# Hybrid attention: probabilities scaled by GpSimd, outputs copied by ScalarE, scores on row halves of the array, values on column halves

## The reference, cut to what matters

```
lg_c = einsum(qa, kc_c) * scale;  p_cmp = masked_softmax(lg_c + bias)    # compressed keys: 15
lg_s = einsum(qa, ks_g) * scale;  p_s   = masked_softmax(lg_s + bias_s)  # selected keys (here all)
lg_w = einsum(qa, kwin) * scale;  p_w   = masked_softmax(lg_w + bias)    # window keys
o_a = g[0] * (p_cmp @ vc_c) + g[1] * (p_s @ vs_g) + g[2] * (p_w @ vwin)
lg_b = where(valid_b, einsum(qb, kbw) * scale + bias_b, NEG)             # banded, with a sink
m = maximum(max(lg_b), sink);  e = exp(lg_b - m)
o_b = (e / (sum(e) + exp(sink - m))) @ vbw
out = concatenate([o_a, o_b]) @ w_out
```

## Time and profile before

| | us |
|---|---|
| time, median of 3 runs | 3504.17 (3500.81 to 3507.8) |
| profiled execution, its own time | 3509.27 |
| its span, from the first instruction to the last | 3507.5 |
| attention stage in it, from the first staging of queries to the first instruction of `out2` | 1849.5 to 2011.18 |
| busy in the span: PE, DVE, ACT, POOL | 2892.5, 1526.5, 452.8, 886.6 |
| mean granted clock of TensorE | 0.903 |

### The profile page before, as it was taken

How to read it: one execution, slowest core, us unless ns; L and a number is a source line. 1 busy time by engine, 2 the same in 40 slices (tenths; PEclk the granted TensorE clock), 3 DMA queues, 4 the chain that set the end, 5 groups by cost and what they waited for, 6 DMA issues and landing times.

```text
span 3507.5 us, 25672 instructions
## 1 busy us (share of the span) xinstructions
PE 2892.5 (82%) x9302; PEld 1717.2 (49%) x9302; DVE 1526.5 (44%) x2316; ACT 452.8 (13%) x1020; POOL 886.6 (25%) x633
## 2 busy tenths in 40 slices
PE   5999887989999999999997899477776666666666
PEld 3444656478888884444456647133332222222222
DVE  5664364122210000001016704765666667767765
ACT  1000232011011010001005501000010001100000
POOL 2111100000000000000000002554556566666663
PEclk9999878999999999999988999798897887888788
DMA  9999420356544443444640045999999999999998
GB/s 380 395 401 341 124 83 15 120 197 222 201 147 155 155 148 140 155 150 137 218 136 1 2 145 218 418 384 417 379 401 422 422 421 422 408 422 422 422 421 355
DMA packets 232373, 922.71 MB, mean 263 GB/s; under 512 B 17819, under 2 KB 37475, under 8 KB 160355
## 3 DMA queue, kind: packets, MB, share of 16 engines
q0 software_dynamic: 99840, 637.57, 44.3%
q1 hardware_dynamic: 132181, 283.96, 23.8%
q10 hardware_dynamic: 272, 0.13, 0.0%
HBM read 918.41 MB, written 8.44 MB: 264 GB/s over the span
## 4 chain that ended last, share of the span: by engine, by line
PE 55%; DMA 25%; DVE 11%; POOL 4%; issue 2%; ACT 2%; DVEq 0%; POOLq 0%; SPq 0%; ACTq 0%
PE ps L1219 17%; PE ps L907 11%; DMA arena<-in_peer_v,proj 10%; PE ps L1245 9%; PE ps L1444 6%; DMA proj<-in_peer_v,proj 4%; DMA proj<-in_peer_u,proj 4%; DMA ring<-in_w_in 3%; DMA arena<-in_w_mod 3%; PE ps L1028 3%; POOL arena L487 3%; PE ps L1421 2%; DVE proj L2049 1%; POOL proj L487 1%; DVE arena L2049 1%
## 5 line engine op out<-in xcount | busy, mean ns | idle before, releaser
L1444 PE MATMUL ps<-proj,gates 128*128 128x512 f32 x992 | 576.0, 745 | 394.2 <-DMA proj<-in_peer_v,proj 272.2
L1219 PE MATMUL ps<-hT,ring 128*128 128x256 f32 x2816 | 608.2, 379 | 1.5 <-ACT hT L526 1.5
L1444 PEld LDWEIGHTS ps<-proj,gates 128*128 128x128 f32 x992 | 233.3, 243 | 733.6 <-issue 604.3
L1219 PEld LDWEIGHTS ps<-hT,ring 128*128 128x128 f32 x2816 | 535.0, 190 | 74.9 <-issue 2.2
L487 POOL DMA_INDIRECT proj<-in_peer_u,proj x128 | 204.8, 1600 | 1427.6 <-DVE proj L2042 1265.1
L907 PE MATMUL ps<-ring,hT 128*128 128x512 f32 (+2 forms) x960 | 381.7, 558 | 8.7 <-DMA ring<-in_w_in 8.7
L2049 DVE CUSTOM_DVE_ANT_0 arena<-arena,yT 128x2048 f32<-128x2048 f32 x128 | 291.5, 2291 | 211.4 <-DMA arena<-in_peer_u,proj 210.9
L2049 DVE CUSTOM_DVE_ANT_0 proj<-proj,yT 128x2048 f32<-128x2048 f32 x128 | 292.1, 2291 | 126.8 <-DMA proj<-in_peer_u,proj 122.7
L1245 PE MATMUL ps<-ring,arena 128*128 128x512 f32 x704 | 304.1, 595 | 2.7 <-ACT arena L725 2.7
L907 PEld LDWEIGHTS ps<-ring,hT 128*128 128x128 f32 x960 | 175.6, 194 | 214.5 <-issue 192.6
L1444 PE MATMUL ps<-arena,gates 128*128 128x512 f32 x512 | 237.3, 607 | 35.9 <-DMA arena<-in_peer_v,proj 35.7
(11 more groups left out here) (410 smaller groups left out, 2568.3 us busy)
## 6 DMA issues: line engine op xcount, KB each, us to landing
arena<-in_w_mod POOLq DMA_DIRECT2D x96, 1024.0 KB, 12.4
ring<-in_w_in SPq DMA_DIRECT2D x52, 1024.0 KB, 12.1
ring<-in_ffn_w_gate SPq DMA_DIRECT2D x44, 1024.0 KB, 5.2
ring<-in_ffn_w_up SPq DMA_DIRECT2D x44, 1024.0 KB, 5.2
ring<-in_ffn_w_down SPq DMA_DIRECT2D x44, 1024.0 KB, 4.8
ring<-in_w_out SPq DMA_DIRECT2D x32, 1024.0 KB, 5.2
ring<-in_peer_wq SPq DMA_DIRECT2D x16, 1024.0 KB, 10.9
ring<-in_w_in SPq DMA_DIRECT2D x16, 960.0 KB, 18.2
```

The source lines that it names most:

```text
L1219: ins = pe.matmul(ps[:, 4 * m + f, 0:T], ring[:, s, k, P * f:P * (f + 1)], hT[:, KS * s + k, :], start=(s == 0 and k == 0), stop=(s == SLO ...
L1444: ins = pe.matmul(ps[:, 4 * t + b, :], diag[:, j, :], row_slots[n % ROWS][:, NB * b:NB * (b + 1)], start=(h == 0 and j == 0), stop=(h == H ...
```

## The change

Five things are changed, all in the attention stage.

- GpSimd takes the multiplication of the probabilities (`scaled`, waits on a new semaphore `att_fac` that `weigh` posts, posts `att_p`), and the staging of the queries (`q_in`).
- ScalarE takes `attended`, after `turned_out` of units 0 and 1 of the next pair; its loop does two pairs per turn, for the two halves of a query buffer that alternates between pairs. `q_out` is one instruction of 128 partitions in place of two of 64.
- The queries of the two heads lie together on 128 partitions, without zeros. A score product uses the row half of its head. Two units are scored together: in `half_scores(u, 0)` the first head of u and the second head of u + 1, in `half_scores(u, 1)` the others, so that the two products of one call go to different halves of the rows and to different banks of PSUM. TensorE waits on its own semaphore `first_half` between the two.
- The products with the values have 64 columns of weights and write to one half of the partitions each, alternating between halves.
- On TensorE all eight pairs are written out, without loops. The queries' tile need not be zeroed (L1903).

```
+        def scaled(i, past, u):
+
+            t, br = UNITS[u]
+            n = {"cmp": (7, 15)[t]}.get(br, P * (t + 1))
+            pool_eng.wait_ge(*at("att_fac", at_unit(i, past, u + 1)))
+            p = hyb["p"][:, u % 4, :, 0:n]
+            pool_eng.tensor_tensor(p, p, hst["sum"][:, u, :].unsqueeze(2).to_broadcast([P, 2, n]), ALU.mult).then_inc(sem("att_p"), 1)
+
+        def head_pair(i, past, more=True):
+            for u in range(NU):
+                scaled(i, past, u)
+                if u == 0 and more:
+                    pool_eng.wait_ge(*(at("att_turned", at_unit(i, past, -3)) if past else at("q_turned", 1)))
+                    q_in(i, past + 1)
...
-        def q_out(k):
-            for h in range(2):
-                r = slice(DK * h, DK * (h + 1))
-                ins = act.activation(hyb["q"][r, k, h, :], ps[r, 4 + k, T:2 * T], ACT.Copy, scale=DK ** -0.5)
-            ins.then_inc(sem("q_out"), 1)
+        def q_out(pair, k):
+            act.activation(hyb["q"][:, pair % 2, k, :], ps[:, 4 + k, T:2 * T], ACT.Copy, scale=DK ** -0.5).then_inc(sem("q_out"), 1)
...
+        def attended(i, past, k, u):
+            act.wait_ge(*at("att_pv", at_unit(i, past, u + 2)))
+            act.copy(yT[:, bass.ds(i + (past + 8 * k), 1), :], ps[:, 6 + k, 0:T].unsqueeze(1)).then_inc(sem("att_out"), 1)
...
+            r = slice(DK * h, DK * (h + 1))
+            ins = pe.matmul(ps[:, u % 4, T * h:T * h + n], hyb["q"][r, (past + u // NU) % 2, int(br == "ban"), P * t:P * (t + 1)], keys[r], start=True, stop=True)
+            if second:
+                ins.then_inc(sem("att_score"), 1)
+            return ins
+
+        def half_scores(i, past, u, n):
+
+            for v, h in (((u, 0), (u + 1, 1)), ((u, 1), (u + 1, 0)))[n]:
+                ins = score(i, past, v, h, n)
+            return ins
...
             for u in range(NU):
-                if u + 4 < NU or more:
-                    score(i, past, u + 4)
+                ahead = u % 2 and (u + 3 < NU or more)
+                if ahead:
+                    half_scores(i, past, u + 3, 0).then_inc(sem("first_half"), 1)
                 turn_p(i, past, u, more)
+                if ahead:
+                    pe.wait_ge(*at("first_half", i * 4 + (4 * past + u // 2 + 3)))
+                    half_scores(i, past, u + 3, 1)
...
             if br == "ban":
                 link(vec.tensor_tensor(s, s, hst["esink"][:, u, :], ALU.add))
-            link(vec.reciprocal(s, s))
-            if br != "ban":
+                link(vec.reciprocal(s, s), "att_fac", wait=False)
+            else:
                 gate = hst["gate"][:, 3 * t + ("cmp", "slc", "win").index(br), bass.ds(i * 2 + 2 * past, 2)]
-                link(vec.tensor_tensor(s, s, gate, ALU.mult))
-            p = hyb["p"][:, u % 4, :, 0:n]
-            link(vec.tensor_tensor(p, p, s.unsqueeze(2).to_broadcast([P, 2, n]), ALU.mult), "att_p", wait=False)
+                link(vec.reciprocal(s, s))
+                link(vec.tensor_tensor(s, s, gate, ALU.mult), "att_fac", wait=False)
```

More of the change, by code:

```diff
@@ L789, in head_pair @@
                 turned_out(i, past, u, more)
+                if u < 2 and past:
+                    attended(i, past - 1, u, NU - 2 + u)
         head_pair(0, 0)
-        with act.Fori(0, 6) as i:
+        with act.Fori(0, 6, 2) as i:
             head_pair(i, 1)
+            head_pair(i, 2)
         head_pair(0, 7, False)
+        for k in range(2):
+            attended(0, 7, k, NU - 2 + k)
         act.wait_ge(*at("att_out", 17))
@@ L1287, in _, with score @@
         pe.wait_ge(*at("kv_out", 1))
-        def score(i, past, u):
+        def score(i, past, u, h, second):
             t, br = UNITS[u % NU]
             g = kv_head(past, u)
-            if past or u >= 4:
+            if not second and (past or u >= 4):
                 pe.wait_ge(*at("att_exp", at_unit(i, past, u - 2)))
-            if u in (NU, NU + 3):
+            if not second and u in (NU, NU + 3):
                 pe.wait_ge(*at("q_out", i * 2 + (2 * past + 3 + u // (NU + 3))))
[L1297 to L1306, removed]
+            if br == "cmp":
+                n = (7, 15)[t]
+                keys = hyb["kc"][:, g, 0:n]
+            else:
+                n = P * (t + 1)
+                keys = hyb["kT"][:, 2 * ("slc", "win", "ban").index(br) + g, 0:n]
+            r = slice(DK * h, DK * (h + 1))
[7 more added lines that the diff above has]
+            return ins
         def turn_q(k):
@@ L1338, in values @@
             dst = ps[:, 7 if br == "ban" else 6, P * t:P * (t + 1)]
[L1339 to L1342, removed]
+            last = br in ("cmp", "ban")
+            for k in range(1 if br == "cmp" else t + 1):
+                for h in range(2):
+                    out = dst[DK * h:DK * (h + 1)]
                     if br == "cmp":
                         n = (7, 15)[t]
-                        v, w = hyb["v_cmp"][0:n, g, cols], hyb["pT"][0:n, u % 2, h, :]
+                        ins = pe.matmul(out, hyb["v_cmp"][0:n, g, DK:2 * DK], hyb["pT"][0:n, u % 2, h, :], start=False, stop=True)
                     else:
-                        v, w = hyb["v"][:, ("slc", "win", "ban").index(br), 2 * k + g, cols], hyb["pT"][:, u % 2, (t + 1) * h + k, :]
-                    ins = pe.matmul(dst, v, w, start=first, stop=(br in ("cmp", "ban") and h == 1 and (br == "cmp" or k == t)))
+                        ins = pe.matmul(out, hyb["v"][:, ("slc", "win", "ban").index(br), 2 * k + g, DK:2 * DK], hyb["pT"][:, u % 2, (t + 1) * h + k, :],
+                                        start=(br in ("slc", "ban") and k == 0), stop=(br == "ban" and k == t))
             ins.then_inc(sem("att_pv"), 1)
@@ L1366, in _ @@
         pe.wait_ge(*at("q_out", 2))
[L1367 to L1376, removed]
+        for u in (0, 2):
+            half_scores(0, 0, u, 0).then_inc(sem("first_half"), 1)
+            pe.wait_ge(*at("first_half", u // 2 + 1))
+            half_scores(0, 0, u, 1)
+        for pair in range(8):
+            head_pair(0, pair, pair < 7)
         values(0, 7, NU - 1)
@@ L1974, in head_pair @@
                     row_max(i, past, u + 3)
-                if u == 0 and more:
-                    vec.wait_ge(*(at("att_turned", at_unit(i, past, -3)) if past else at("q_turned", 1)))
-                    q_in(i, past + 1)
-                if u == 1 and past:
-                    attended(i, past - 1, 1, NU - 1)
-            attended(i, past, 0, NU - 2)
         vec.wait_ge(*at("bias_in", 16))
-        q_in(0, 0)
         for u in range(3):
```

31 lines of the change are left out of this document (15 added, 16 removed).

## The result

The kernel with the change took 3545.49 us, the median of 4 runs (3542.6 to 3549.32); the kernel before, beside it, 3505.91 (3500.81 to 3507.8). The ratio is 1.0116, 95% interval 1.0098 to 1.0133: slower by 39.6 us. The forecast was 3530, range 3508 to 3550. The way it moved and the relay were right; the size was +26 in place of +39.6. The time lies near the upper edge of the range: just outside the 3514 to 3545 that the forecast's own terms allow, inside only because the range reached towards the rival with a low clock throughout.

A forecast was written before the change was run, and what follows sets the result against it. VectorE's queue was taken as the bound, TensorE close behind. Pairs +4.1, +14.5 and +1.9, start -2.2 gave +18.3 us; low clock +8 made +26, so 3504.2 + 26 = 3530, range 3508 to 3550.

The forecast's parts named there:

- the relay: Attention pairs: four times, VectorE waits for scores behind TensorE's turn, which waits for GpSimd's multiplication; 9.5 us a pair.
- rival with a low clock throughout: Attention stage: relays plus TensorE at its low clock throughout, +43 us, 3547; chance 0.18.
- VectorE is relieved, and waits instead: Attention pairs: VectorE loses 7.1 us of work a pair, but idles before its bias step, about 75 us in all.
- The relay's price at full clock: Units 1, 3, 5, 7: handovers, GpSimd multiplication, turn and two passes cost 2.19, 1.92, 2.52, 2.46 us.
- Turn and scores do not flow into each other: TensorE in relays: scores start only when the turn has ended, not 0.16 earlier; a tiling change costs 0.18 us.
- The halves overlap, and it does not help: TensorE's scores: overlapping row halves give nothing in relays, since the head VectorE waits for is issued first.
- The clock: Attention pairs: TensorE busy 65% at most, so half the pairs' time at the low level, +8 us, bounds 0 and 17.
- First halves in the way of the turns: TensorE: values, first halves and even turns lie beside VectorE's 12.9 us and cost nothing at full clock.
- price at the low clock: Attention pairs: the four relays grow by 0.6, 0.3, 0.65 and 0.55 at the low level, 2.1 us a pair.
- No change: Rival: handovers of 0.05 and no drain make relays about 7.2 us, close to the 7.1 taken away; 3500 to 3508, chance 0.12.
- faster: Rival: GpSimd at VectorE's speed, short handovers and no drain make relays 4.9 us a pair; 3488, chance 0.08.
- the halves run one after the other: TensorE's array halves do not overlap; stays hidden and gives the same 3530; no separate chance.

The follow-up runs named there:

- e2: Kernel before plus only the moves to GpSimd and ScalarE; TensorE's full-width products and order as before: 3461.83 us, ratio 0.9879.
- e7: e2's kernel with scores of the next two units made only after the turn behind units 1, 5, 7, full width: 3513.19 us, ratio 1.0025.
- e5: e2's kernel with the values multiplied in column halves, scores still full: 3459.69 us, ratio 0.9878 to the kernel before.
- e1: Changed kernel with both halves of the scores issued ahead of the turn of unit u: 3517.34 us, ratio 1.0038 to the kernel before.
- e6: e1's kernel with values back to full width, row halves of the scores kept: 3506.69 us, ratio 1.0003 to the kernel before.

## Why the prediction was right, and where its size was off

**VectorE is relieved, and waits instead.** Right. VectorE's idle time at the bias step behind scores was forecast at about 75 us, 1.8 to 3 each; it was 92.9 us in 30 waits over the whole stage, 2.2 to 3.9 each (the first scores of the stage, which are no relay, not counted). The relief was forecast at 7.1 us a pair; e2 shows 20.0 - 14.1 = 5.9, with 0.7 of waits for scores left. The 20.0 held 0.4 that came from the loop's first pair alone; the others took 19.3 to 19.7.

**The relay's price at full clock.** Right, as far as it can be told. The change's own relays were never seen at full clock; e7 gives 2.38 to 2.54 in its cleanest pair for relays that by the same parts, with a whole unit's scores, were priced at 2.62 to 2.74. The parts, against the forecast: handover from VectorE to GpSimd 0.08 (0.15), from GpSimd to TensorE 0.15 (0.15); GpSimd's multiplication 0.61 and 1.04 (0.73 and 1.05); the two copies of `q_in` 0.74 together (0.8), so `scaled(1)` was on time.

**Turn and scores do not flow into each other.** The prediction took 0.18 from one row for the change between full and part of the array. e5 and e7, both at full clock, tell it better: two turns of `128*7` or `128*128` and then values start 0.22 apart where all is full width, 0.31 apart where the values are in column halves.

```profile
1921.88 0.38 PE L1362 MATMUL ps<-tab,proj 128*7 128x128 f32 x2 [0.91 <-POOL proj L496]
1922.10 0.61 PE L1384 MATMUL ps<-arena 128*128 128x128 f32 x4
```
```profile
1896.41 0.38 PE L1361 MATMUL ps<-tab,proj 128*128 128x128 f32 x2
1896.72 0.66 PE L1382 MATMUL ps<-arena 128*64 128x128 f32 x8
```

The 0.09 is half of what was taken. (The prediction counts 32 such changes in relays; by its own count of relays they are 30. The sum does not use it.) The Trainium skill, TensorEngine Tiling (Array Packing), section Key Properties, has the rule that a change of tiling mode drains TensorE: the trace agrees in direction. In the change itself, at the low clock, the scores start 0.07 ahead of the turn's end (1941.61 against 1940.57 + 1.11), where the prediction had 0, and 0.16 in a row of equal ones.

**The halves overlap, and it does not help.** e1's eight passes of 256 columns in row halves took 2.52 us at the low clock, against 1.91 for four at full width, so two units take 2.52 in place of some 3.8 (an estimate, twice the 1.91). The prediction said that this stays out of VectorE's way, since the head it waits for is first. Right.

**The clock: the step that failed.** The prediction reasoned from the busy share ("65% at most") to "half of the pairs' time at the low level: +8, bounds 0 and 17". TensorE had the low level nearly throughout (0.52 over seven pairs, five of them at 0.50), so the term was near its upper bound. The reasoning was too short as well: it has the clock follow from how busy TensorE is, and expects a slow TensorE, being a busy one, to be granted more again. In e1 it was busy 91% and stayed at 0.56; in e7, without halves, busy 77%, it had 0.88. And with the same order as e1's, the values at full width alone bring 0.56 to 0.84 (e6). So the busy share alone does not foresee the clock, and which products run matters too; the prediction did not consider that. Whether 65% at full width would have cost the clock in this stage, no run tests: there TensorE was never busy less than 74% of a pair in the loop. Elsewhere in the kernel before, 480 to 500 us, it had 58% and 0.64. What the low clock costs was in the rival of a low clock throughout, priced at +43 and given 0.18. Its time, 3547, is within 2 us of what was measured: the rival describes this result better than the forecast does.

**First halves in the way of the turns: priced at nothing.** "TensorE's other work (values, first halves, even turns) lies beside VectorE's 12.9 us and costs nothing at full clock". At the low clock it does cost: the turn of unit 1 started 0.61 later than it could, that of unit 7 0.25 (GpSimd done at 1946.34, turn at 1946.74). The rival had it, at 1 us a pair.

**The sum, mended.** In the loop the forecast was 22.4 + 1.05 = 23.45 us a pair, measured 25.7. Of the 2.2 between them, 1.05 is the other half of the clock's term; 0.9 is the relays' excess over their price at the low clock (2.44, the mean of 2.20 and 2.67, with 3.46, 3.28 and 3.30 are 12.5 against 11.6), which is the first halves; 0.3 is VectorE's own work beside the relays. Six pairs: 13.4 us. The first pair is 1.1 over its forecast with half a clock's term, and the last pair with the tail some 3, since its two relays, turns and values ran at 1.2 GHz too. With the start's -0.5 that is 17 us, the 43.3 - 26 of the stage.

**The other rivals.** No change and faster fell: relays are 2.2 us and more, GpSimd is about as slow as its rows said. That the halves run one after the other falls too, by the 2.52 above.

## What to carry to other kernels

- A unit of work may be moved to an idle engine only if nobody waits for the way there and back. Look at what the relieved engine does next, and behind what that stands in the third engine's queue: here the order `score(u + 4)` ahead of `turn_p(u)` makes the same moves worth -43 us (e2), and three relays a pair take all of it back (e7, 9 us above the kernel before). To issue it ahead of the turn of the same unit is not enough if the turn of the unit before still stands in its way (e1, e6).
- Fewer and shorter instructions on the array are not a gain by themselves: look at the granted clock of the stretch afterwards. Packing into halves of both kinds saved passes' time and came with the low clock, with TensorE as busy as before.
- Test a change of several parts part by part. The best kernels here (e5, 3459.69, and e2, 3461.83, not told apart) are parts of this change.

## What the runs showed of the hardware that was not expected

- TensorE busy 81% of 178 us was granted 0.52, and in e1, busy 91% of 153 us, 0.56; in another order with full-width products it was busy 77% and granted 0.88 (e7). Column halves beside full scores left it at 1.00 (e5). Which property of the products does it stays open.
- A VectorE instruction of two columns was held for the length of a GpSimd multiplication, in the kernel with the change, in the last pair: 1.02 us in place of 0.16.

```profile
2041.51 0.16 DVE L1992 RECIPROCAL vrows<-vrows 128x2 f32<-128x2 f32 x1
2041.71 1.02 DVE L1993 TENSOR_TENSOR vrows<-vrows 128x2 f32<-128x2 f32 x1
```
```profile
2041.68 1.37 POOL L496 TENSOR_TENSOR proj<-proj,vrows 128x512 f32<-128x512 f32 x2 [1.08 <-DVE vrows L1993]
```

The Trainium skill, SBUF — State Buffer, section Who interferes with whom, says that a VectorE instruction with two inputs in SBUF contends with a GpSimd instruction that reads SBUF. This trace agrees: VectorE's instruction ends at 2042.73, and GpSimd's row is two multiplications, the first of them 1.04 long, so until 2042.72. It is the only hold of this length in the stage. The 0.3 us a pair that the prediction estimated for `q_in`'s copies are about 0.1: a step of `row_max(3)` took 0.25 beside them (at 1951.08), in place of 0.16.
